# Waits by bank between output projections and gate and up units, and another order of the border between sublayers

## The reference

```
def ffn_sublayer(h, m, sub, g_pre, g_post, w1, w2):
    shift, scale, gate = mods_of(m, sub)
    y = swiglu(modulate(rms_norm(h, g_pre[sub]), shift, scale), w1, w2)
    return h + MACARON_WEIGHT * gate * rms_norm(y, g_post[sub])

def hybrid_layer(x, xc, ...):
    x = ffn_sublayer(x, mod, 0, ...)
    xc = ffn_sublayer(xc, mod_c, 0, ...)
    # neighbourhood attention, window attention and a Fourier mix of both streams, then @ w_out
    x = x + gt * rms_norm(o, g_post[1])
    x = ffn_sublayer(x, mod, 2, ...)
    ...
```

## Time and profile before

| | before |
|---|---|
| median of 3 runs | 3916.86 us (3916.53 to 3919.34) |
| the profiled execution | 3917.44 us, of which the span of its instructions 3915.6 us |
| busy, share of the span | TensorE 94%, VectorE 42%, ScalarE 31%, GpSimd 26% |
| mean granted clock of TensorE | 0.971 |

### The profile page before, as it was taken

One profiled execution on the slowest core, in us unless ns is written; L12 is line 12 of the kernel. 1 busy time (PEld: TensorE's weight loads), 2 busy tenths in 40 slices (PEclk: granted clock), 3 DMA queues, 4 the chain that ended last, 5 costly groups with the idle time before them and its releaser, 6 DMA issues.

```text
span 3915.6 us, 53761 instructions
## 1 busy us (share of the span) xinstructions
PE 3676.8 (94%) x20615; PEld 3035.8 (78%) x20615; DVE 1625.2 (42%) x2378; ACT 1210.3 (31%) x1895; POOL 1013.1 (26%) x419
## 2 busy tenths in 40 slices
PE   7999999988999999999999988899999899979998
PEld 4888887855788888788888776677888789679756
DVE  5555444167334342335343325631225544551134
ACT  3212123147331111331211323642223523321363
POOL 1332222200122232223223221034443133023301
PEclk9999999999999999999999999999998999789999
DMA  5333332210123323223333221023332123012201
GB/s 199 126 124 126 100 109 88 62 42 1 54 81 113 97 91 97 66 80 109 100 113 98 64 94 56 17 70 95 93 97 89 41 80 92 1 54 87 75 1 54
DMA packets 88423, 316.73 MB, mean 81 GB/s; under 512 B 10576, under 2 KB 11856, under 8 KB 87632
## 3 DMA queue, kind: packets, MB, share of 16 engines
q1 hardware_dynamic: 85200, 300.22, 24.4%
q10 hardware_dynamic: 3072, 14.40, 1.0%
HBM read 312.49 MB, written 2.10 MB: 80 GB/s over the span
## 4 chain that ended last, share of the span: by engine, by line
issue 66%; POOL 17%; PE 16%; ACT 1%; DVE 1%; POOLq 0%; DVEq 0%; ACTq 0%
POOL w_parts L516 17%; PE psum L1735 9%; PE psum L2118 1%; PE psum L2134 1%; PE psum L2143 1%; PE psum L2022 1%; PE psum L2052 0%; PE psum L2041 0%; PE psum L2122 0%; PE psum L2057 0%; PE psum L2032 0%; ACT sb_weight L894 0%; PE psum L2157 0%; POOLq L515 0%; PE psum L2066 0%
## 5 line engine op out<-in xcount | busy, mean ns | idle before, releaser
L1735 PE MATMUL psum<-h_parts,w_parts 128*128 128x512 f32 (+1 forms) x11760 | 2019.8, 334 | 64.9 <-POOL w_parts L516 16.5
L1735 PEld LDWEIGHTS psum<-h_parts,w_parts 128*128 128x128 f32 x11760 | 1780.1, 189 | 300.0 <-issue 58.6
L516 POOL TENSOR_TENSOR w_parts<-w_raw,w_parts 128x1024 fp32r<-128x1024 f32 x415 | 1012.9, 2441 | 2889.2 <-ACT w_parts L538 2889.2
L538 ACT ACTIVATE w_parts<-w_raw 128x1024 fp32r<-128x1024 f32 x415 | 439.8, 1060 | 2106.7 <-PE psum L1735 1480.0
L1751 PE MATMUL psum<-w_parts,hidden_parts 128*128 128x512 f32 x2904 | 663.9, 390 | 21.7 <-DVE to_split L1110 19.7
L1751 PEld LDWEIGHTS psum<-w_parts,hidden_parts 128*128 128x128 f32 x2904 | 545.1, 188 | 139.6 <-issue 23.6
L1110 DVE TENSOR_TENSOR to_split<-silu_gate,psum 128x768 f32<-128x768 f32 (+1 forms) x88 | 78.1, 888 | 767.1 <-PE psum L1735 767.1
L962 DVE TENSOR_TENSOR hidden_parts<-to_split,hidden_parts 128x768 f32 (+1 forms) x88 | 185.9, 2113 | 100.8 <-ACT hidden_parts L543 100.8
L1073 DVE SCALAR_TENSOR_TENSOR mod_products<-mod_ring,cond_rows 128x1024 bf16<-128x1024 f32 x128 | 179.1, 1399 | 79.4 <-DMA mod_ring<-modw_dram 76.5
L1075 DVE SCALAR_TENSOR_TENSOR mod_ring<-mod_ring,cond_rows 128x1024 f32<-128x1024 f32 x128 | 210.5, 1644 | 0.0
L1040 DVE TENSOR_TENSOR y_tok<-y_tok,psum 128x512 f32 (+1 forms) x88 | 59.6, 688 | 245.5 <-PE psum L1751 245.5
(11 more groups left out here) (299 smaller groups left out, 2792.5 us busy)
## 6 DMA issues: line engine op xcount, KB each, us to landing
w_raw<-wu_dram SPq DMA_DIRECT2D x415, 512.0 KB, 3.6
mod_ring<-modw_dram SPq DMA_DIRECT2D x128, 512.0 KB, 4.2
na_bias<-rpb_dram ACTq DMA_DIRECT2D x6, 896.0 KB, 4.7
four_dft<-four_dram ACTq DMA_DIRECT2D x2, 2048.0 KB, 7.5
mod_first_k<-modw_dram SPq DMA_DIRECT2D x7, 512.0 KB, 9.9
mod_first_b<-modw_dram SPq DMA_DIRECT2D x5, 512.0 KB, 10.7
mod_first<-modw_dram SPq DMA_DIRECT2D x4, 512.0 KB, 7.6
resid<-xT_dram SPq DMA_DIRECT2D x1, 2048.0 KB, 13.5
```

The costliest lines, as they stand in the source:

```text
L516: pool.tensor_tensor(SPL[:, s % 2, 1], RAW[:, s % 2], SPL[:, s % 2, 0].bitcast(F32), ALU.subtract).then_inc(w_split, 1)
L538: act.activation(SPL[:, u % 2, 0], RAW[:, u % 2], ACT.Copy).then_inc(w_hi, 1)
L1735: ins = pe.matmul(PS[:, pair, PSO[a]:PSO[a] + z - a], SPL[:, s, wp, k], src[:, xp, k, t0 + a:t0 + z], start=k == 0 and n_ == 0, stop=k == ...
```

## The change

Three things change, all in the order of instructions and in what they wait for.

The projections' waits move into the first unit, ahead of token tiles 0, 2 and 4, one entry of the list for each pair of banks. The next part's four units wait for as many banks as they write, by pair. For the mixing sublayer the projection's single wait is repeated for each pair, so that it still stands ahead of all.

At the border TensorE makes all eight sums of part A after part A's turns, where seven stood one by one between turns from the sixth group on. The columns of part A stand after part B's first group of turns, and its spreading after the last one, ahead of all sums of part B. ScalarE's root of part A stands right after the eight squares of part A, and VectorE's reciprocal after part B's fourth update instead of its fifth. The very first entry, ahead of sublayer 0, stays as it was.

```diff
                         act.activation(SQE[:, m, a:z], XT[:, m, META + a:META + z], ACT.Square).then_inc(esq_ready, 1)
-                        if hi == 1 and m == 2:
+                        if hi == 0 and m == DT - 1 and before is not None or hi == 1 and m == 2 and before is None:
                             entry_root(sub, 0)
...
-                        if after is not None and hi == 1 and m == 4:
+                        if after is not None and hi == 1 and m == 3:
                             entry_recip(after, 0)
...
-            def entry_stats(sub, spread=True):
-
-                idx = subs.index(sub)
+            def entry_sums_a(sub):
+
+                for m in range(DT):
+                    entry_sum(sub, 0, m)
+
+            def entry_stats(sub, first):
+
                 for hi, (a, z) in enumerate(sub["halves"]):
-                    for m in range(subs[idx - 1]["sums"] if idx > 0 and hi == 0 else 0, DT):
-                        if hi == 1 and m == 2:
+                    if hi == 0 and not first:
+                        continue
+                    for m in range(DT):
+                        if hi == 1 and m == 2 and first:
                             entry_cols(sub, 0)
-                        if hi == 1 and m == 4 and spread:
-                            entry_rows(sub, 0)
                         entry_sum(sub, hi, m)
...
-            def out_unit(u, i, j, src, T, KT, yb, ready, cap):
+            def out_unit(u, i, j, src, T, KT, yb, ready, cap, entry):
...
                 for t in range(n):
+                    if entry is not None and t % 2 == 0:
+                        pe.wait_ge(*entry[t // 2])
                     if j % 4 == 0:
...
             def out_units(u, src, T, KT, entry, ready, yb, cap=DT):
 
-                for semaphore, value in entry:
-                    pe.wait_ge(semaphore, value)
                 with pe.Fori(0, 2) as i:
                     for j in range(4):
-                        out_unit(u, i, j, src, T, KT, yb, ready, cap)
+                        out_unit(u, i, j, src, T, KT, yb, ready, cap, entry if j == 0 else None)
...
-                for semaphore, value in entry:
-                    pe.wait_ge(semaphore, value)
                 for j in range(DT):
-                    out_unit(u, 0, j, src, T, KT, sub["yb"], ready, cap)
+                    out_unit(u, 0, j, src, T, KT, sub["yb"], ready, cap, entry if j == 0 else None)
...
                     ins.then_inc(yt_ready, 1)
-                    if after is not None and g >= 5:
-                        entry_sum(after, 0, g - 5)
-                sub["sums"] = max(0, len(groups) - 5)
+                    if after is not None and g == n_a - 1:
+                        entry_sums_a(after)
+                    if after is not None and g == n_a:
+                        entry_cols(after, 0)
+                if after is not None:
+                    entry_rows(after, 0)
...
-                    entry = [(bank_read, yb)] * 4
+                    entry = [(bank_read, yb - T // P + min(2 * p + 2, T // P)) for p in range(4)]
...
-                last_out_units(sub, u + 16, H, DT, [(v_ready, e + 6)], e, cap=6)
+                last_out_units(sub, u + 16, H, DT, [(v_ready, e + 6)] * 3, e, cap=6)
```

More of the change, by code:

```diff
@@ L1775, in last_out_units @@
                 groups = sub["groups"]
+                n_a = sum(x[0] == 0 for x in groups)
                 for g, (hi, a, z, ms, bk) in enumerate(groups):
@@ L2181, in _ @@
                 T = sub["T"]
-                entry_stats(sub, spread=idx > 0)
+                entry_stats(sub, first=idx == 0)
                 if idx == 0:
```

## The result

The changed kernel takes 3880.36 us (median of 4 runs, 3875.81 to 3882.50) beside 3918.10 us before (4 runs of the same chip): ratio 0.9902, 95% interval 0.9885 to 0.9919. The forecast was 3872 us, with a range of 3862 to 3887. A second set of runs of the same kernel (e4) gave 0.9906. The times alone can't say whether the missing 7 us of 44.7 are real; the lengths of stages in the profile can.

A forecast was written before the change was run, and what follows sets the result against it. TensorE, busy 94% of the span, was taken as the bound. Waits 31.6, borders 11.2 + 0.4 and clock 1.5 sum to 44.7 us off 3917.4; with the median 0.6 lower, 3872 us, range 3862 to 3887.

The forecast's parts named there:

- Waits by banks: Feed-forward projections and gate and up units: all 20 TensorE waits for VectorE go, worth 31.6 us.
- The loops' entry: Projection loops: the sequencer runs ahead, so entry costs nothing; exposed, 16 entries of 0.26 us would cost 4.2 us.
- The stall: Eight looped projection entries: the wait returns as loading of loop code, 3889 us; a rival with chance 0.06.
- The border: Between sublayers: VectorE's entry pass starts 3.0 us sooner; four 768-token borders give 11.2 us, the 512-token one 0.4.
- each cover: At the border: squares, part A's root and the reciprocal lie under other TensorE work, so nothing waits for them.
- Part B's root: At the border, in ScalarE's queue: it can't start before the later sums end; ScalarE up to 1.4 us late, priced 0.2.
- The clock: At one of twelve projection entries: the low-clock spell behind the wait disappears, worth 1.5 us.
- a rule for each of them: At all 20 waits: each small idle time costs a clock spell, 30 us together; rival at 3844 us, chance 0.02.
- so all 20 waits go: 28.4 us: Projections and gate and up units: idle time removed, 19.7 + 4.4 + 4.3 us.
- the border gives nothing: Between sublayers: ScalarE's late root or longer waits of turns consume the gain, 3883 us; a rival with chance 0.12.
- Rival 4: At borders: lightly loaded sums drop the clock to 1.2 GHz, up to 14 us each, 3928 us; chance 0.03.

The follow-up runs named there:

- e4: The changed kernel, unaltered, measured again on the chip of e1 to e3: 3882.98 us, ratio 0.9906.
- e11: Kernel before, only with the 512- and 256-column widths alternating from weight part to weight part, as in e6: 3910.71 us, ratio 0.9983.
- e7: Kernel after, but part A's sums stand behind turn groups from the sixth on, as before, with columns and spreading directly behind them: 3896.87 us, ratio 0.9951.
- e8: Kernel after, but part A's columns stand behind the second of part B's sums and the spreading behind the fourth: 3887.31 us, ratio 0.9922.
- e2: Kernel after with the old waits of projections and units restored, leaving only the new border: 3904.42 us, ratio 0.9965.
- e6: Kernel after, but gate and up widths alternate from weight part to weight part (512, 256, then 256, 512): 3860.85 us, ratio 0.9855.
- e5: Kernel after, but every 768-token gate and up unit multiplies 256 columns before 512 under each weight part: 3875.33 us, ratio 0.9898.
- e1: Kernel before with all new waits by bank, the border left as it was: 3892.38 us, ratio 0.9936.
- e3: Kernel after, but the gate and up units wait for all banks of the projections again: 3882.24 us, ratio 0.9906.
- e9: Kernel of e6, but the gate and up units wait for all banks of the projections again: 3875.01 us, ratio 0.9896.
- e10: Kernel of e6, with ScalarE loading the SiLU activation table at the start of each feed-forward sublayer: 3856.54 us, ratio 0.9849.

## Why the prediction was right, and where it wasn't

**Waits by banks: mechanism right, size slightly low.** All 20 are gone, none came back. Where the stages have one pace they are worth 33.3 us where I had 31.6 (the table of e11): closing a gap gives about 0.25 us more than the idle time shown and not 0.16.

**The loops' entry: right.** The sequencer reaches it 2.9 us ahead, and in the feed-forward sublayers L1757 has no wait that isn't for weights. (In the two mixing sublayers it waits 2.3 us in all for VectorE at L1251; before, the same two waits stood there as "issue", 2.2 us.) The stall that "Runtime: NRT & Kernel Launch", section "Instruction fetch mechanics", of the Trainium skill made conceivable shows at none of the eight entries: the idle time there is 0.

**The border: right, slightly low.** Four give 12.0 us where I had 11.2, the fifth 0.75 where I had 0.4. The pass starts 3.3 us sooner (forecast 3.0) with each cover in its place; e7 and e8 show what two of them are worth. Part B's root does wait now (1.38 us), as forecast.

**The clock: the spell went, its gain didn't come.** All three kernels with waits for L1110 (before, e2, e11) have one spell of a low clock behind one of their twelve waits, and the ten without them have none in any projection, so that mechanism held. But spells came elsewhere: before has another one in its first looped stage (0.986 over that stage), after has two in or next to first units behind borders (a mean of 0.83 over 1066 to 1076 and of 0.79 over 1656 to 1664, which costs 1.7 us of matmuls each), so nothing of the 1.5 us is left. "TensorE: Matmul & The Clock Gate", "A second HAM failure mode: psum-queue depth-cycling", of the Trainium skill, speaks of small idle times that come frequently; I had read it as a rule for each of them. That reading isn't borne out here: the gaps lie 45 to 138 us apart within a sublayer, and without them the mean clock is 0.972 after 0.971.

**What failed is a step that wasn't there.** The term "so all 20 waits go: 28.4 us" priced a wait by its idle time alone and took the units behind it as unchanged. They changed: without a wait ahead of them all stages behind projections ran at the slow pace. That puts the kernel after 8.5 us above the sum, shown by stage lengths in all profiles and by e11 against e6. The measured time fell inside the range partly by luck: waits and borders gave 2.8 us more than I had (33.3 and 12.7 instead of 31.6 and 11.6), the clock 1.5 less, and the range had been made wide for other reasons. With these sizes the sum is 33.3 + 12.7 - 8.5 = 37.5 us, where 37.6 were measured. The rival "the border gives nothing" would have given a time near the measured one (3883) for a wrong reason; the borders' stretches exclude it. Rival 4, "slower", was priced too low by its own rows: some 28 us of nearly full TensorE work at half the clock cost up to 28 us more and not 14. The clock stayed at 1.00 there, so nothing came of it.

**Open.** What inside TensorE makes two patterns of one loop, and why a wait ahead lets it fall to the quick one in 13 cases of 18, isn't settled. e5 only excludes that the order of the widths within a pair decides it, and the stages of 14 and 10 units show that behind a wait it can differ between executions of one kernel.

## What to carry to other kernels

A wait's idle time is the price of removing it only if the work behind it keeps its pace: compare the mean of the same instruction form, stage by stage, before and after, not only the waits. Where matmuls of two widths alternate, try the order in which two of one width follow each other; here that one line was worth 19 us on the kernel after, about half of what the change gave, and 7 us on the kernel before. And move short sums and roots where the next engine has other work in front of it: early sums and early spreading gave 1.4 and 0.4 us alone and 3.3 together.

## What the runs showed of the hardware

- A loop of float32 matmuls of 512 and 256 columns, with a weight load for each, ran at 347 or 353 ns a pair at full clock, fixed for a whole stage of 100 to 136 us. Of stages that began without a wait all 36 (after, e1, e4, e5, e7, e8) were slow; of those behind a wait of 1.1 us 13 of 18 (before, e2, e3) were quick, and of the stages of 14 and 10 units behind 0.8 to 2.4 us 11 of 36.
- In the order 512, 256, 256, 512 (a mean of 348 ns for 512 and 256 together) the looped stages had one length in all 24 cases (e6, e9, e10, e11), with a wait ahead or without.
- 512 columns alone have one pace: 0.227 us a matmul in the projections of every kernel.
- The two profiles of the kernel after (after, e4) differ by 9 us in span, mostly behind the six sublayers, with 219 and 242 us at 1.2 GHz, while their looped stages behind projections agree within 0.1 us.
- ScalarE's load of a table took 1.28 us; e6 has 32 of them for the copy of the weights and SiLU, and with one load ahead of each feed-forward sublayer (e10) 4 are left.
